# First round of a section: the third unit takes one block with every tile from the second on

## The reference, cut to what matters

```python
def _swiglu(h, w_in, w_out):
    gate, up = jnp.split(h @ w_in, 2, axis=-1)
    return (jax.nn.silu(gate) * up) @ w_out
...
    for i in range(DEPTH):
        g = norm_gains[i]
        h = h + 0.5 * _rmsnorm(_swiglu(_rmsnorm(h, g[0, 0]), ffn_w_in[i, 0], ffn_w_out[i, 0]), g[0, 1])
        u = _rmsnorm(h, g[1, 0])
        ...
        h = h + _rmsnorm(m, g[1, 1])
        h = h + 0.5 * _rmsnorm(_swiglu(_rmsnorm(h, g[2, 0]), ffn_w_in[i, 1], ffn_w_out[i, 1]), g[2, 1])
```

## Time and profile before

| | |
|---|---|
| median of 3 runs | 2321.19 us (2319.07 to 2324.08) |
| profiled execution | 2317.64 us |
| its span, first to last instruction | 2315.8 us |
| TensorE busy | 2229.2 us, 96% of the span |
| GpSimd busy | 1700.1 us, 73% |
| ScalarE, VectorE busy | 1051.1 us, 910.7 us |
| mean granted TensorE clock | 0.995 of full speed |

### The profile page before, as it was taken

How to read it: one execution, slowest core, us unless ns; L and a number is a source line. 1 busy time by engine, 2 the same in 40 slices (tenths; PEclk the granted TensorE clock), 3 DMA queues, 4 the chain that set the end, 5 groups by cost and what they waited for, 6 DMA issues and landing times. The chain is left out here.

```text
span 2315.8 us, 54229 instructions
## 1 busy us (share of the span) xinstructions
PE 2229.2 (96%) x20672; PEld 2165.8 (94%) x20672; DVE 910.7 (39%) x1917; ACT 1051.1 (45%) x1549; POOL 1700.1 (73%) x1306
## 2 busy tenths in 40 slices
PE   9999999999999899999999898789999999999998
PEld 8999999999999779999999898669999999999997
DVE  4322334323330544322431987734322431344332
ACT  5344545444443545444444573335344444465442
POOL 6887758887887738887888403738887888757996
PEclk9999999999999999999999999999999999999999
DMA  6563544554564315564655342015564655444662
GB/s 218 171 196 123 157 128 152 174 196 130 180 189 152 128 65 155 173 199 126 181 186 177 100 155 66 3 45 167 172 197 130 182 182 181 145 124 124 191 207 99
DMA packets 90124, 348.80 MB, mean 151 GB/s; under 512 B 10016, under 2 KB 11808, under 8 KB 90016
## 3 DMA queue, kind: packets, MB, share of 16 engines
q1 hardware_dynamic: 90016, 347.31, 47.5%
HBM read 346.22 MB, written 1.05 MB: 150 GB/s over the span
## 5 line engine op out<-in xcount | busy, mean ns | idle before, releaser
L1693 POOL TENSOR_TENSOR w_lo<-raw,w_hi 128x512 fp32r<-128x512 f32 (+4 forms) x1124 | 1545.7, 1408 | 412.2 <-ACT w_hi L1186 392.6
L339 PE MATMUL bank<-x_hi,w_hi 128*128 128x272 f32 (+1 forms) x3264 | 945.7, 290 | 4.1 <-DVE x_lo L1833 2.8
L341 PE MATMUL bank<-x_hi,w_lo 128*128 128x272 f32 (+1 forms) x3264 | 941.7, 289 | 0.0
L340 PE MATMUL bank<-x_lo,w_hi 128*128 128x272 f32 (+1 forms) x3264 | 937.6, 287 | 0.0
L1186 ACT ACTIVATE w_hi<-raw 128x1024 fp32r<-128x1024 f32 (+2 forms) x608 | 678.7, 1119 | 385.0 <-PE bank L341 368.4
L339 PEld LDWEIGHTS bank<-x_hi,w_hi 128*128 128x128 f32 x3264 | 615.1, 188 | 7.7 <-DVE hid_lo L1971 2.7
L340 PEld LDWEIGHTS bank<-x_lo,w_hi 128*128 128x128 f32 x3264 | 615.5, 189 | 0.1
L341 PEld LDWEIGHTS bank<-x_hi,w_lo 128*128 128x128 f32 x3264 | 615.0, 188 | 0.0
L339 PE MATMUL bank<-hid_hi,w_hi 128*128 128x272 f32 (+1 forms) x1408 | 404.1, 287 | 0.0
L341 PE MATMUL bank<-hid_hi,w_lo 128*128 128x272 f32 (+1 forms) x1408 | 403.7, 287 | 0.0
L340 PE MATMUL bank<-hid_lo,w_hi 128*128 128x272 f32 (+1 forms) x1408 | 403.0, 286 | 0.0
(11 more groups left out here) (377 smaller groups left out, 2352.6 us busy)
## 6 DMA issues: line engine op xcount, KB each, us to landing
raw<-in_ffn_in SPq DMA_DIRECT2D x352, 512.0 KB, 3.5
raw<-in_ffn_out SPq DMA_DIRECT2D x128, 704.0 KB, 4.1
raw<-in_sb_in SPq DMA_DIRECT2D x48, 512.0 KB, 3.5
raw<-in_rw_in SPq DMA_DIRECT2D x24, 512.0 KB, 3.2
raw<-in_sb_out SPq DMA_DIRECT2D x16, 512.0 KB, 3.5
raw<-in_mla_out SPq DMA_DIRECT2D x8, 512.0 KB, 3.2
raw<-in_rw_lora SPq DMA_DIRECT2D x8, 512.0 KB, 3.2
raw<-in_rw_out SPq DMA_DIRECT2D x8, 512.0 KB, 3.4
```

The lines of the kernel that those rows point to most:

```text
L339: nc.tensor.matmul(o, wh, xh[:, k, cols()], start=start, stop=False)
L340: nc.tensor.matmul(o, wh, xl[:, k, cols()], start=False, stop=False)
L341: last = nc.tensor.matmul(o, wl, xh[:, k, cols()], start=False, stop=stop)
L1693: part = nc.gpsimd.tensor_tensor(w_lo[:, s, w], raw[:, s, w], w_hi[:, s, w], ALU.subtract)
```

## The change

One expression and one condition in `first_round` change. Unit 2 takes a block after the high parts of each tile from the second on (the block of the tile before it), so that seven of its eight blocks are issued between tiles; the eighth heads the rest. Only TensorE's order changes, in nine first rounds (seven of `in`, two of `q`); the number of instructions stays the same on each engine, and the other engines' programs are the same. The position of `input_sum` is counted in blocks of the rest, and its constant isn't changed.

```diff
-                early, c = DT_ // 2 if behind_norm and sec.start else 0, cols()
+                early, c = DT_ - 1 if behind_norm and sec.start else 0, cols()
...
-                    if early and k % 2:
-                        block_of_unit(2, k // 2)
+                    if early and k:
+                        block_of_unit(2, k - 1)
```

## The result

The change makes the kernel slower, by 0.37%: 2332.39 us (2327.59 to 2333.14, 6 runs) against 2322.74 us of the kernel before on the same chip (2319.07 to 2326.01, 6 runs), ratio 1.0037, 95% interval 1.0027 to 1.0047. A second measurement on another occasion (run r1) gave 1.0030, 1.0017 to 1.0042. The forecast was 8.3 us or 0.36%.

A forecast was written before the change was run, and what follows sets the result against it. TensorE was taken as the bound, busy 2229.2 of 2315.8 us. Terms 6.8 + 1.06 + 0.54 - 0.1 gave 8.3 us, laid on the median 2321.19: 2329.5 us, 0.36% slower, range 2324 to 2334.

The forecast's parts named there:

- No pause between the tiles to fill: Nine first rounds, TensorE between tiles: moved blocks fill nothing in eight rounds, gain 0; the ninth has 0.64 us at its sum.
- The sum moved behind nine matmuls: First rounds: the sum and the chain behind it start 1.13 us later, 6.8 us over six `in` rounds, 1.06 in the last.
- Two waits, for bank 0 and for bank 1: Round 2 of each `in` section: TensorE waits 0.7 us before the first unit; the second is 1.13 us late together.
- Units 0 and 1 end later, cost 0 beside the sum: First rounds: units 0 and 1 end 1.13 us later, delaying their weights; cost 0, or 0.1 us a round without cover.
- `q` of layer 0: Round after layer 0's `q` first round: bank 0 comes free 1.13 us later, so TensorE loses 0.54 us.
- `q` of layer 3: Sum in layer 3's `q`: extra matmuls fill the wait for `acc`, sum 0 to 0.26 us later; gain 0.1 us taken.
- Part hidden: Rival on the chain behind the sum: slack hides part of the loss, 5.9 us, or 4 us if half hidden; chance 0.10.
- Faster: Rival at the tiles: waits are longer than the rows show and new blocks fill them, 7 us gained, 2314; chance 0.04.
- Clock: Rival at the two new pauses: they lower TensorE's granted clock, 12 us on top, 2341; chance 0.03.
- Weights: Rival at GpSimd's four halves: late weights push slots 2 and 3 too, at most 0.3 us a round more, 2332; chance 0.05.

The follow-up runs named there:

- r1: The changed kernel measured once more, unaltered, for a second profile and more times; ratio 1.0030, span 2328.7 us.
- e5: The kernel before without any block of unit 2 between the tiles, the sum behind as many matmuls as before; ratio 1.0047.
- e2: The kernel before with only the sum three blocks (nine matmuls) later, four blocks between the tiles as before; ratio 1.0042.
- e1: The changed kernel with the sum back at its old place in TensorE's stream, seven blocks still between the tiles; ratio 1.0011 over the kernel before.
- e8: The kernel before with only the sum five blocks (15 matmuls) later; ratio 1.0058.
- r2: The kernel before profiled once more, unaltered; span 2319.6 us.
- e9: The kernel before with one added wait: in layer 3's `q`, GpSimd's first `w_lo` waits for VectorE's `acc`; one profile, sum at 10.15 us, second unit at 15.57.

## Why the prediction was right

*No pause between the tiles to fill.* Right for eight rounds, by e5 and by the distances: the four blocks fill the tiles' delay, three more gain 0. Wrong for layer 3's `q`, where the prediction went by idle times of 0.0: three more gain 0.31 us at the sum there.

*The sum moved behind nine matmuls.* Right in mechanism and size. 1.15 us was measured per `in` round for 1.13 said, 1.04 for 1.06 in the last. e2 alone makes the loss, e1 takes most of it away, e8 gives it a slope.

*Two waits, for bank 0 and for bank 1.* Right: 0.76 us at the first unit and 0.40 more at the second. The forecast of 0.7 for the second counted 0.3 that was there before.

*Units 0 and 1 end later, cost 0 beside the sum.* Right as a sum. With that cover gone the prediction had 0.1 us a round, for GpSimd's `w_lo`. e1 shows 0.10 us at the first unit, as said (0.35 in the last `in` round), but 0.25 at the second, and this larger part the prediction left out: it comes from ScalarE, whose root stands behind `w_hi` of slots 0 and 1.

*`q` of layer 0.* 0.71 us for 0.54. VectorE begins to take out bank 0 at 13.15 in the round for 12.02, 1.13 us later, just as said. But TensorE starts 0.15 us behind the end of that instruction where 0.05 was assumed, so the first unit is 0.64 late, and the first matmuls after the pause are slower: from the first unit to the second it is 3.10 us where it was 3.03.

*`q` of layer 3.* The size was near, -0.16 for -0.1, and that is luck, for the reason was wrong. The prediction took the pause at the sum for TensorE being early and let nine more matmuls fill it, with the sum 0 to 0.26 us later. The pause was VectorE's add, held up by GpSimd. In the changed kernel units 0 and 1 end later, so GpSimd starts later and the two don't meet, and `acc` is there 1.1 us before TensorE comes to the sum. The sum starts at 10.90 where it was 10.92: 1.06 us for the nine matmuls, less the 0.77 us of the wait, less 0.31 us of pauses between the tiles, which had been put at nothing. Had the sum stood at its old place, the round would have gained 0.85 us, as e1 has it.

*The rivals.* Part hidden: fell, there is no slack. Faster: fell. Clock: the distances of the `in` rounds of both kernels repeat in their second profiles, at a full clock, so the pauses cost only themselves there. But the first profile's span grew by 14.4 us, not by 8.5. r1 and r2 put 9.1 us between the kernels, and both intervals of the ratio hold 8.5 us, so the 5.9 us beyond it are put down to the spread between executions, which a second profile of the kernel before shows too. Weights: no row of the changed kernel's `in` rounds has TensorE wait for them.

What stays open is whether the two new pauses change anything in how often the clock falls later. In the stretch with the RWKV mixer both profiles of the changed kernel had more of the lower clock than both of the kernel before, but e8 less than one of these; the data are too scattered to say.

## What to carry to other kernels

A position that is counted in steps of a list moves when the list does: whoever shortens the front of a hand-written order should look for every mark that is counted from it. A short instruction whose result a long chain of other engines waits for (here one sum) should be placed by that chain, and the filling be put behind it. Before more filler goes in, take the present filler out once in an experiment: it tells what there is to fill. And where matmuls overlap, look for pauses in the distance of two starts and not in the idle times alone: in layer 3's `q` these read 0.0 where 0.31 us were lost.

## What the runs showed of the hardware

VectorE's add of two 128x272 tiles took 1.56 us in place of 0.44 when GpSimd's two-input operation began 0.02 us before it, that is until 0.29 us after the end of GpSimd's first half of 1.29 us. The Trainium skill (SBUF — State Buffer, SBUF: two separate sides) says that VectorE, with two inputs in SBUF, and a GpSimd instruction that reads SBUF need the same pair of ports, that whichever starts first holds it for the whole instruction, and that the other is blocked. This trace agrees. e9, in which GpSimd is kept back, shows the cause, and in e5, where units 0 and 1 end early, GpSimd begins 0.30 us before the add in the `in` round of the table and the add takes 1.42 us there. In the gate-and-up rounds of the kernel before GpSimd begins its `w_lo` at 561.17, 0.06 us behind VectorE's add. The add takes 0.44 us there, and it is GpSimd's first half that is longer, 1.52 us for 1.29. So 0.08 us in the order of two starts is worth 1.1 us of VectorE's time.
